# A hybrid encoder layer on one core: RWKV tiles rolled through three slots, FFN down projection in 512-wide matmuls, attention scores negated

## What is computed

```python
aq, ak, av, bq, bk, bv, cin = split(rmsnorm(x) @ w_in)
o_win  = window_gqa(aq, ak, av)               # +-128 tokens
s = bq @ bk.T * 64**-0.5 - slope * |i - j|    # 4 heads x 2 maps
o_diff = (softmax(s[0]) - lam * softmax(s[1])) @ bv
o_rwkv = rwkv7_bidir(cin)                     # one scan per direction:
#   S = S*w - (S kk) kk_a + v k;  y = S r
x = x + concat(o_win, o_diff, o_rwkv) @ w_out
x = x + cross_attn(rmsnorm(x), mem)
gate, up = split(rmsnorm(x) @ w_gu)           # w_gu 1024 x 5632
x = x + (silu(gate) * up) @ w_down            # w_down 2816 x 1024
out = rmsnorm(x)
```

## Time and profile before

| | |
|---|---|
| median of three runs | 1998.86 us |
| profiled execution | 1994.96 us, span 1993.2 us |
| granted TensorE clock, mean | 0.955 |
| PE / PEld / DVE / ACT / POOL busy | 90 / 79 / 38 / 31 / 29 % |
| instructions | 36710 |

### The profile page before, as it was taken

One profiled execution on the slowest core, in us unless ns is written; L12 is line 12 of the kernel. 1 busy time (PEld: TensorE's weight loads), 2 busy tenths in 40 slices (PEclk: granted clock), 3 DMA queues, 4 the chain that ended last, 5 costly groups with the idle time before them and its releaser, 6 DMA issues.

```text
span 1993.2 us, 36710 instructions
## 1 busy us (share of the span) xinstructions
PE 1787.5 (90%) x15985; PEld 1569.9 (79%) x15985; DVE 762.1 (38%) x1275; ACT 619.5 (31%) x1208; POOL 573.0 (29%) x530
## 2 busy tenths in 40 slices
PE   5998988899776893888999887999999999999997
PEld 4897777678655882887998787888998899889987
DVE  4004998333165558455323235111331133113315
ACT  5113887322255222223215434211111111111112
POOL 3222663131045334335225101122222222222220
PEclk9998999999878996998999997999999999999998
DMA  5120000021000000000513010121111111111112
GB/s 163 54 65 1 1 1 1 22 69 37 16 1 5 4 4 1 4 4 17 185 38 106 27 37 22 38 59 48 49 48 48 48 48 48 47 49 48 47 39 85
DMA packets 67727, 81.52 MB, mean 41 GB/s; under 512 B 4594, under 2 KB 62992, under 8 KB 67568
## 3 DMA queue, kind: packets, MB, share of 16 engines
q1 hardware_dynamic: 66624, 76.60, 12.5%
q0 software_dynamic: 944, 2.58, 0.5%
HBM read 74.96 MB, written 4.19 MB: 40 GB/s over the span
## 4 chain that ended last, share of the span: by engine, by line
PE 76%; DVE 14%; ACT 5%; POOL 2%; issue 2%; DMA 2%; DVEq 0%; ACTq 0%; POOLq 0%; SPq 0%
PE PS L1401 12%; PE PS L1402 12%; PE PS L1404 12%; PE PS L1638 8%; PE PS L1414 8%; PE PS L1416 7%; PE PS L1415 7%; PE PS L1496 2%; DVE E__69 L984 2%; PE PS L1530 1%; PE PS L1522 1%; DVE E__69 L1012 1%; DVE XN L910 1%; DVE s_QQ L1217 1%; DMA XT<-in_x 1%
## 5 line engine op out<-in xcount | busy, mean ns | idle before, releaser
L400 POOL TENSOR_TENSOR WL<-RAW,WH 128x512 fp32r<-128x512 f32 x228 | 309.7, 1366 | 975.0 <-ACT WH L532 975.0
L1401 PE MATMUL PS<-HH,WH 128*128 128x512 f32 x1072 | 421.9, 394 | 11.4 <-POOL WL L400 8.9
L1402 PE MATMUL PS<-HL,WH 128*128 128x512 f32 x1072 | 420.8, 393 | 0.0
L532 ACT ACTIVATE WH<-RAW 128x512 fp32r<-128x512 f32 x228 | 141.5, 631 | 694.8 <-PE PS L1404 332.9
L1404 PE MATMUL PS<-HH,WL 128*128 128x512 f32 x1072 | 333.2, 392 | 0.0
L1401 PEld LDWEIGHTS PS<-HH,WH 128*128 128x128 f32 x1072 | 203.8, 190 | 54.5 <-issue 8.3
L1414 PE MATMUL PS<-WH,AH 128*128 128x256 f32 x864 | 244.9, 283 | 1.4 <-DVE AL L1322 1.4
L1415 PE MATMUL PS<-WL,AH 128*128 128x256 f32 x864 | 244.5, 283 | 0.0
L1416 PE MATMUL PS<-WH,AL 128*128 128x256 f32 x864 | 244.5, 283 | 0.0
L1404 PEld LDWEIGHTS PS<-HH,WL 128*128 128x128 f32 x1072 | 203.3, 190 | 42.8
L1402 PEld LDWEIGHTS PS<-HL,WH 128*128 128x128 f32 x1072 | 203.5, 190 | 41.9
(11 more groups left out here) (289 smaller groups left out, 2680.4 us busy)
## 6 DMA issues: line engine op xcount, KB each, us to landing
RAW<-in_ffn_w_gu SPq DMA_DIRECT2D x88, 256.0 KB, 2.8
RAW<-in_w_in SPq DMA_DIRECT2D x48, 256.0 KB, 2.7
RAW<-in_ffn_w_down SPq DMA_DIRECT2D x44, 256.0 KB, 2.9
XT<-in_x SPq DMA_DIRECT2D x8, 512.0 KB, 8.3
RAW<-in_w_out SPq DMA_DIRECT2D x16, 256.0 KB, 3.8
X<-in_x SPq DMA_DIRECT2D x8, 512.0 KB, 7.4
RAW<-in_x_wkv SPq DMA_DIRECT2D x16, 256.0 KB, 3.0
out_x<-FO SPq DMA_DIRECT2D x8, 512.0 KB, 2.6
```

The lines of the kernel that those rows point to most:

```text
L400: pool.tensor_tensor(WL[:, p % NW], RAW[:, p % NRAW], WH[:, p % NW].bitcast(F32), ALU.subtract).then_inc(w_lo, 1)
L532: act.activation(WH[:, p % NW], RAW[:, p % NRAW], ACT.Copy).then_inc(w_hi, 1)
L1401: pe.matmul(where(ct, i), wh[:, k, c], ah(kt)[:, t0:t0 + n], start=first and starts(ct, i), stop=False, skip_group_check=True)
L1402: pe.matmul(where(ct, i), wh[:, k, c], al(kt)[:, t0:t0 + n], start=False, stop=False, skip_group_check=True)
```

## The change

RWKV: three slots with two PSUM banks each, and bank 6 for the chain and bank 7 for the front of a tile are shared. A direction runs ten periods. In a period p the newest tile is put through its front and level 0, the one before it through levels 1 and 2 and the first product of 3, the one before that through the rest, and the chain is advanced for the one before that. All engines follow that order. Transposes come in two parts, four after the gram products and two after the system. FFN down: a piece of w_down is 128 rows x 512 columns, products stream 512 columns, one bank for each token tile and half, and the last down runs tile by tile. Attention: BQ and TAB are negated, DVE takes a minimum, exp has scale -1, and the negation instruction with its two waits is gone; before TAB is rescaled DVE waits for its last read.

```diff
         class Slot:
-            def __init__(self, i):
-                b, n = 172.25 * i, f"s{i}_"
-                self.bank = 4 * i
+            def __init__(self, i, b, b2):
+                n = f"s{i}_"
+                self.a, self.b = 2 * i, 2 * i + 1
...
-        slots = [Slot(0), Slot(1)]
+        slots = [Slot(0, 0, 10), Slot(1, 172.25, 182.25), Slot(2, 186.25, 132)]
+        NS = len(slots)
+        CHAIN, FRONT = 6, 7
...
-                pieces += [(w_dn, (i - 1) * PW, c0) for c0 in range(0, D, PW)]
+                pieces += [(w_dn, (i - 1) * PW + k * P, h * 512) for h in range(2) for k in range(2)]
...
+        def jobs_at(d, p):
+            return [Job(d, p - age) if 0 <= p - age < NT else None for age in range(4)]
...
@@ gpsimd
+                for p in range(NT + 2):
+                    new, mid, old, done = jobs_at(d, p)
+                    if mid:
+                        coupling(mid, 2)
+                    if new:
+                        coupling(new, 0)
+                        system_t(new)
+                    if mid:
+                        coupling(mid, 3)
+                    if new:
+                        coupling(new, 1)
+                    if mid:
+                        coupling(mid, 4)
...
@@ scalar
-                        act.activation(BQ[:, k, t0:t0 + 512], bank[i], ACT.Copy, scale=0.125).then_inc(job_evac, 1)
+                        act.activation(BQ[:, k, t0:t0 + 512], bank[i], ACT.Copy, scale=-0.125).then_inc(job_evac, 1)
...
-                    act.wait_ge(nm_done, 2 * u + i + 1)
+                    act.wait_ge(s_read, 2 * u + i + 1)
...
-                    act.activation(e, e, ACT.Exp, bias=NMD[:, n % 4:n % 4 + 1], accum_out=LD[:, n % 4:n % 4 + 1]).then_inc(exp_done, 1)
+                    act.activation(e, e, ACT.Exp, bias=MD[:, n % 4:n % 4 + 1], scale=-1.0, accum_out=LD[:, n % 4:n % 4 + 1]).then_inc(exp_done, 1)
...
@@ vector
                 if qb == 0 and h:
+                    dve.wait_ge(s_read, 2 * u)
                     link(TS(TAB[:, :], TAB[:, :], DIFF_SLOPES[h] / DIFF_SLOPES[h - 1], None, ALU.mult))
...
-                    ins.then_inc(s_read, 1)
-                    dve.wait_ge(s_read, 2 * u + i + 1)
-                    TS(NMD[:, n % 4:n % 4 + 1], MD[:, n % 4:n % 4 + 1], -1.0, None, ALU.mult).then_inc(nm_done, 1)
...
+                for p in range(NT + 2):
+                    new, mid, old, done = jobs_at(d, p)
+                    k = p - 3
+                    if old:
+                        inverse(old, 3)
+                    if new:
+                        gram(new)
+                    if mid:
+                        inverse(mid, 1)
+                    if new:
+                        system(new)
+                    if old:
+                        inverse(old, 4)
+                    if done:
+                        if k == 0:
+                            chain_first(done)
                         else:
+                            chain_step(2 * k)
+                    if mid:
+                        inverse(mid, 2)
+                    if done:
+                        add_y(done, k)
+                    if old:
+                        results(old)
+                    if done:
+                        chain_step(2 * k + 1)
+                    if new:
+                        inverse(new, 0)
...
+                    for tt in range(NT):
+                        for h in range(2):
+                            dve.wait_ge(f_mm, 14 * (i - 1) + 2 * tt + h + 1)
+                            xs = X[:, tt, 512 * h:512 * h + 512]
+                            dve.wait_ge(f_add, 16 * (i - 2) + 8 * h + tt + 1)
+                            TT(xs, PS[:, (2 * tt + h) % 8, :], xs, ALU.add).then_inc(f_add, 1)
+                        if tt:
+                            final(tt - 1)
+                    final(NT - 1)
...
@@ tensor
+                for p in range(NT + 2):
+                    new, mid, old, done = jobs_at(d, p)
+                    k = p - 3
+                    if old:
+                        inverse(old, 3)
+                    if mid:
+                        xx(mid, 1)
+                    if new:
+                        gram(new)
+                    if old:
+                        xx(old, 4)
+                    if mid:
+                        inverse(mid, 1)
+                    if new:
+                        system(new)
+                    if old:
+                        inverse(old, 4)
+                    if mid:
+                        xx(mid, 2)
+                    if done and k:
+                        pe.wait_ge(g_dve[done.i], done.dve0 + DVE_OUT)
+                        chain_step(2 * k)
+                    if old:
+                        wu(old)
+                    if mid:
+                        inverse(mid, 2)
+                    if new:
+                        xx(new, 0)
+                    if done:
+                        state_out(done, k)
+                    if old:
+                        results(old)
+                    if mid:
+                        xx(mid, 3)
+                    if done:
+                        pe.wait_ge(y_add, NT * d + k + 1)
+                        chain_step(2 * k + 1)
+                    if new:
+                        inverse(new, 0)
...
+                    def down_mm(bank, wh, wl, k, tt):
+                        t, a = slice(tt * P, tt * P + P), 2 * (m % 2) + k
+                        pe.matmul(PS[:, bank, :], AH[:, a, t], wh, start=k == 0, stop=False, skip_group_check=True)
+                        pe.matmul(PS[:, bank, :], AH[:, a, t], wl, start=False, stop=False, skip_group_check=True)
+                        return pe.matmul(PS[:, bank, :], AL[:, a, t], wh, start=False, stop=k == 1, skip_group_check=True)
...
+                    for h in range(2):
+                        ws = [wide(take()) for _ in range(2)]
+                        for tt in range(NT):
+                            n = 8 * h + tt
+                            if n < 4:
+                                pe.wait_ge(f_silu, 4 * i + n + 1)
+                            elif n < 8:
+                                pe.wait_ge(f_mul, 4 * i + n - 4 + 1)
+                            else:
+                                pe.wait_ge(f_add, 16 * m + n - 8 + 1)
+                            for k in range(2):
+                                mm = down_mm(n % 8, *ws[k], k, tt)
```

More of the change, by code:

```diff
@@ new lines, in gram @@
+                def gram(j):
+                    sl = j.slot
+                    dve.wait_ge(g_pe[j.i], j.pe0 + PE_GRAM)
+                    for hp in range(2):
+                        ins = TT(sl.G[:, :, hp:4:2, 0:2, :].rearrange("p a u r t -> p a u (r t)"),
+                                 PS[:, (sl.a, sl.b)[hp], :].rearrange("p (a u c) -> p a u c", a=2, u=2),
+                                 MK[:, d, 0:2 * C].unsqueeze(1).unsqueeze(1).broadcast_to([P, 2, 2, 2 * C]), ALU.mult)
+                    ins.then_inc(g_dve[j.i], 1)
@@ L1683, in _, with both, units, gram @@
+                def both(t, t4, i, ct):
+                    return t4[:, i, ct, 2 * t:2 * t + 2, :].rearrange("p c k -> p (c k)")
+                def units():
+                    return [(u, c, slice(64 * c, 64 * c + 64)) for u in range(4) for c in range(2)]
+                def gram(j):
+                    sl, t = j.slot, j.tile
+                    pe.wait_ge(g_dve[j.i], j.dve0)
+                    for kind in range(2):
                         for ct in range(2):
                             for hp, c in QUADS:
-                                r = slice(64 * hp, 64 * hp + 64)
@@ new lines, in gram, with system @@
+                    for kind in range(2):
+                        for ct in range(2):
+                            f = 256 * kind + P * ct
+                            mm = pe.transpose(PS[:, FRONT, f:f + P], both(t, BKt, kind, ct), ID)
+                    mm.then_inc(g_pe[j.i], 1)
+                def system(j):
+                    sl, t = j.slot, j.tile
+                    pe.wait_ge(g_dve[j.i], j.dve0 + DVE_GRAM)
+                    for ct in range(2):
+                        for hp, c in QUADS:
+                            r = slice(64 * hp, 64 * hp + 64)
+                            mm = mm1(PS[64 * c:64 * c + 64, (sl.a, sl.b)[hp], 64 * ct:64 * ct + 64], KR[r, 0, ct, 2 * t + c, :], BKt[r, 0, ct, 2 * t + c, :])
+                    mm.then_inc(g_pe[j.i], 1)
+                    pe.wait_ge(g_act[j.i], j.act0 + ACT_KEYS)
+                    for ct in range(2):
+                        pe.transpose(PS[:, FRONT, P * ct:P * ct + P], both(t, KR, 0, ct), ID)
+                    for u, c, r in units():
+                        mm = mm1(PS[r, FRONT, 256 + 64 * u:320 + 64 * u], sl.G[r, 1, u, 0, :], VT[r, t, 64 * u:64 * u + 64])
+                    mm.then_inc(g_pe[j.i], 1)
@@ new lines, in xx, with inverse @@
+                def xx(j, l):
+                    sl = j.slot
```

(40 more changed lines are left out.)

445 lines of the change are left out of this document (182 added, 263 removed).

## The result

The changed kernel takes **1951.46 us** (median of four runs, 1949.14 to 1951.98) against 1998.27 us (four runs, 1996.33 to 2001.79) for the kernel before: a ratio of 0.9762, 95% interval [0.9745, 0.9778], or 46.8 us less. Five later runs gave 1950.06 us, a ratio of 0.9757 [0.9733, 0.9781]. The forecast was 1968.0 us with a range of 1956 to 1982.

The account below looks back on a forecast made before the run. PE, busy 90% of 1993.2 us, was taken to bound the kernel. FFN -19.2, RWKV -8 and attention -3.3 gave -30.5 on the profiled 1994.96: 1964.5, plus 3.9 to the median, forecast 1968 us, range 1956 to 1982.

Parts of the forecast that it names:

- FFN, -19.2: FFN: 512-wide down matmuls save 12.5 us over ten iterations, the tail done tile by tile saves 6.7.
- The rivals of 0.238 us and of double cost: FFN down: wide matmuls start every 0.238 us (1979, chance 0.03), or cost twice the narrow (1981, chance 0.05).
- RWKV, -8: RWKV scan: -4 over both directions, -3.3 at the end of direction 1, -0.7 after direction 0.
- Period: 12.5 + 0.8 + 0.15 + 0.4 = 13.9: Full RWKV period in us: PE work 12.5, waits for DVE 0.8, extra turns 0.15, issue waits 0.4; 14.9 before.
- The stalls of 0.8: RWKV period: PE waits about 0.4 us before XX of level 1 and about 0.4 before WU, both for DVE's adds.
- The unnamed waits of weight loads: RWKV: unnamed issue waits, 7.1 us a direction; half lies in waits that go, so 0.4 a tile stays.
- The sum of 119 us: RWKV direction: ten periods, five of them full and the others filling or draining, 119 us against 121.3 before.
- Attention, -3.3: Attention: removing the negations saves 3.3 us, after 0.15 for three new waits; ends 0 and -9.6.
- In the chain I count 25 of them: Attention: 25 of the 64 negations of 0.15 us lie in the critical chain, 3.3 us together.
- The 3.9 us from execution to median: Whole kernel: the median of the runs lies 3.9 us above the profiled execution, added to turn 1964.5 into 1968.
- the strong case: Rival: PE takes over all of the RWKV stage with no stall (-16), attention gives -5: 1958; chance 0.10.
- The low clock while filling: RWKV rival: PE stays at 1.2 GHz while slots fill; two slow periods 1984 (chance 0.10), slower overall from three (0.04).

Follow-up runs that it names:

- The equal rows with 20 matmuls more: Kernel before and attention part alone, each with 20 extra 512-wide matmuls before the projections behind attention: 1996.13 and 1987.40 us, preparation and windows 94.3 us in both.
- the second with four buffers: Changed kernel with four output buffers instead of two in the tail, run a second time beside the changed kernel: 1951.44 us, ratio 0.976.

## Why the prediction missed its range

- **What bounds the kernel:** right, PE does, and the FFN grid is what I read from the earlier trace rows.
- **FFN, -19.2:** measured -19.6 alone, with 21.8 us for a down, the first scale at 7.9 and the last at 27.4, each as walked. The rivals of 0.238 us and of double cost fall.
- **RWKV, -8:** measured -15.8 alone. The failed step is "Period: 12.5 + 0.8 + 0.15 + 0.4 = 13.9". It measured 12.93. The floor and the turns were right. The stalls of 0.8 were not: in five periods PE's own row has 0.2 us of waits, and its weight loads wait 0.8 us for DVE. I priced the two waits as if a product followed its add directly, but by then PE has gram products, the system and another tile's products in its order. The unnamed waits of weight loads did not go with the rounds, 2.4 us in the five periods are still there, but they cost PE little: of 0.8 + 0.4 = 1.2 the period holds 0.2 to 0.3, what is left beyond 12.5 and the turns. The sum of 119 us used 13.8 for a full period (119 less 50 for the other five, over five); 12.93 instead, in ten full periods of the two directions, is 8 to 9 us, which is the miss. Beside it smaller errors cancel. The end of direction 1 takes 893.93 - 891.75 = 2.2 us where the earlier trace rows had 6.4 and I had 3.1. Direction 0's scan took 113.5 and direction 1's 120.1: to the third mask 19.9 and 23.5 us, as the granted clock was 0.91 there in the one and 0.69 in the other, and behind the last mask 29.8 and 32.8, where direction 1's stretch also holds the last chain step.
- **Attention, -3.3:** measured -11.4 alone. The failed step is "In the chain I count 25 of them": the chain passes through one engine at a time, but the delay was in every unit's loop, and a unit shortened by some 0.15 us over 32 units. That gives about 5 (189.7 to 184.6). (By its own terms, 3.3 and 0.02 to issue for each of 25, less 0.15, the forecast would have been 3.65.) The rest, some 6 us, I had no term for: about 4 of them lie in the projections and the preparation, where the code did not change, and I read these as where the clock falls. The equal rows with 20 matmuls more support that; it is not shown for good, and about 2 us stay open.
- **The 3.9 us from execution to median:** right for the kernel before, whose first profiled execution was a short one, but no property of both kernels. The profiled executions of the kernel before took 1994.96, 2000.55 and 2001.89 us, while the changed kernel's took 1951.89 and 1949.35 against medians of 1951.46 and 1950.06. From first profile to first profile the change is 43.1 us, by medians 46.8.
- **The rivals:** the strong case (PE takes over all of RWKV with no stall, -16, attention -5), at a chance of 0.10, came closest: RWKV gave 15.8 and attention's own stage 5. Its 1958 still lacked the rest of what the attention part gave. The low clock while filling came in part: direction 1's first two periods took 3.6 us more than direction 0's, at 0.69, where the kernel before had 0.87 in its first 20 us. In another profile, the second with four buffers, the two took 17.8 us from mask to mask, as in direction 0, and not 21.4 as here, so this is chance from run to run. It is less than the 8 us of the rival's two slow periods. The minimum costs what the maximum did, 1.22 us.

## What to carry to other kernels

When several tiles are interleaved on one engine, price a wait between two dependent steps only after laying the engine's own order between them; a stall that other work covers is worth nothing. A small instruction in a loop that two engines share is worth its effect on the unit's period times the units, and not the times it shows up in the critical chain. Where an engine's clock is below full over a stage, the stage's length has a few microseconds that depend on timing alone: look at more than one profile of the kernel before, and put that into the range.

## What the hardware showed that I had not expected

- PE work that nobody needs can be free or better: 20 matmuls in a wait of 5.8 us for weights left the end of that wait where it was and made the products behind it start 0.23 instead of 0.43 us apart; 10 matmuls did not. Over the whole kernel nothing of it was left (1996.13 us in one run, 1987.40 with the new attention form).
- The same kernel's attention stage took 232.9, 232.2 and 238.3 us in three executions, with a mean granted clock over attention itself of 0.97 in the first and 0.93 in the last; the runs of the kernel before lie between 1992.5 and 2004.9 us.
- One more change from 64-wide to 128-wide use of the array and back costs 0.19 to 0.25 us within a period of 12.9. The Trainium skill (TensorEngine Tiling (Array Packing), Key Properties) names a drain without a figure; these periods are in line with it.
